# A layer of gated linear attention and SwiGLU: o of three heads in four turned through DRAM and by VectorE's 32 by 32 blocks instead of on TensorE

## The chip, the cores and the metric

One core of one Trainium2 chip. The metric is the device time of one execution in microseconds (us). Matrix products run on TensorE (PE in the profile), the rest on VectorE (DVE), ScalarE (ACT) and GpSimd (POOL); SyncE (SP) and ScalarE issue the DMA transfers.

## The reference

One layer on 2048 tokens of width 1024, in float32, cut to what the change touches:

```
hn = rmsnorm(h)
q, k, v, r, a_low = split(hn @ w_in)              # 4 heads, dk 128, dv 256
log_a = log_sigmoid(a_low @ w_a2 + b_a) / 16      # cumulated in chunks of 64 tokens
o = scores(q, k, decays) @ v + (q * decays) @ state      # by chunks, state carried on
o = rmsnorm(o of each head) * silu(r)
h = h + o.reshape(seq, 1024) @ w_out
h = h + (silu(g) * u) @ w_down      with g, u = split(rmsnorm(h) @ w_gu)
out = rmsnorm(h)
```

## The kernel before, in words

Numbers are kept as two float32r parts, hi and lo, and a product takes three matmuls (`three`, lines 735 to 737). The mixer goes over NB = 4 blocks of T = 512 tokens, each over H = 4 heads; then two stages of seven-product schemes make the feed-forward layer. The change lies in the mixer, which lasts until about 890 us, but for a few lines at the very end.

Weights of the mixer come through a ring: a block has 16 rounds of four units of 128x512. SP loads `raw` by pairs of units (`load_pair`, issue on line 405), each pair after GpSimd has split the same pair of the round before. GpSimd makes `ring_hi` and `ring_lo` of a unit (lines 660 and 663) after TensorE has used that unit of the round before. Head hd has rounds 3 hd (q and k columns), 3 hd + 1 and 3 hd + 2 (v and r, two halves); rounds 12 to 15 are w_out.

TensorE's order for heads 0 to 2: `make_scores` (k turned, past and future scores), the second half of v and r as four `vr_unit`s, the q columns of the next head, then, after the silu of r has read the banks (`r_silu`), `use_scores` with two units of the next head's v and r between, the k columns, `vr_unit` 2, `turn_o` (eight transposes of `og` into banks 6 and 7, line 878), `vr_unit` 3. Head 3 has no next head: `use_scores` follows on v and r, needing only the first `v_done`, and its `turn_o` lies inside the product with w_out.

VectorE's order for one head (`head`, from line 1685): k_lo, two predicated copies into `scores` (line 1698), scores_lo, the work of `under_vr`, state_in of the first tile (line 1708), two v_lo, the gate, the states, `under_o`, the root, four `og` tiles (line 1729); then `scale_qk` of the next head (lines 1611 to 1617) and `turned_o_lo`. ScalarE's order: k_hi, two copies into `scores`, scores_hi, `under_vr`, two v_hi, the silu of r (line 1210), the squares and the root, the decays, `turned_o_hi`. Under v and r of heads 1 and 2 lie, for blocks after the first, three operand splits of the block before: ScalarE issues two stores to xop (line 1161), splits three granules into three `x_stage` buffers, each after that buffer's last store has landed, and VectorE makes their low parts. Under v and r of head 3 lie, but for the last block, four squares of the next x on ScalarE, a root, and one scaled tile on VectorE. Between heads all orders are written out by hand; every engine goes strictly in its own.

SP also loads x of the next block in head 3 (line 461, blocks 1 and 2, after a wait for all xop stores) and the first feed-forward weights in heads 1 and 2 of block 3 (line 421).

```
def load_pair(i, p, parts):
    if i > 0:
        sp.wait_ge(unit_split[2 * p], i)
        sp.wait_ge(unit_split[2 * p + 1], i)
```

## Time and profile before

| what | value |
|---|---|
| median of 3 runs | 2199.96 us (2193.34 to 2200.28) |
| the profiled execution's own time | 2198.29 us |
| its span | 2196.6 us |
| granted TensorE clock, mean | 0.997 |
| TensorE busy | 2149.8 us |
| VectorE, ScalarE, GpSimd busy | 1384.1, 823.6, 1630.0 us |

The span goes from the first to the last instruction of the program. A row of a timeline has start, duration, engine and line, operation, what is written and read, and in brackets the idle time of its engine before it with what ended it. Merged rows have a count; their duration is that of the whole run of them.

### The profile page before, as it was taken

The page shows a single profiled execution, that of the slowest core. Times are in us where ns is not written, and L with a number is a line of the kernel's source. Part 1 is how long each engine was busy: PE and PEld are TensorE (multiplying, and loading weights), DVE is VectorE, ACT ScalarE, POOL GpSimd, SP SyncE. Part 2 cuts the span into 40 slices and gives each one's busy share as a digit, 9 for nine tenths or more (in the row PEclk, how much of TensorE's full clock was granted, in tenths as well). Part 3 has the DMA queues.
Part 4 walks back from the last instruction along what each step waited for, and adds up shares of the span by engine and source line. Part 5 has one row for each costly group of instructions (what it writes and reads, how often), then busy time and mean ns, then how long its engine had stood idle before and what let it go on. Part 6 is the DMA issues. An engine that isn't in the chain of part 4 may idle for free.

```text
span 2196.6 us, 27842 instructions
## 1 busy us (share of the span) xinstructions
PE 2149.8 (98%) x9922; PEld 1776.9 (81%) x9922; DVE 1384.1 (63%) x1800; ACT 823.6 (37%) x1461; POOL 1630.0 (74%) x1294
## 2 busy tenths in 40 slices
PE   8999999999999999999999998999999999999997
PEld 6888888778878888778888877888888878888885
DVE  6445644554455453378787855757667567978786
ACT  4333433343344333344444433443434422142223
POOL 7646675667566765788888878888888887878784
PEclk9999999999999999999999999999999999999999
DMA  6222354335433655745545458443434588759782
GB/s 187 77 67 87 121 186 121 119 114 189 123 131 110 200 162 201 259 158 201 182 175 192 161 206 344 151 166 135 171 132 174 206 308 311 282 214 359 262 320 105
DMA packets 225545, 404.75 MB, mean 184 GB/s; under 512 B 17184, under 2 KB 156448, under 8 KB 216448
## 3 DMA queue, kind: packets, MB, share of 16 engines
q1 hardware_dynamic: 190448, 360.44, 46.0%
q10 hardware_dynamic: 34960, 42.54, 5.8%
q8 instruction: 79, 1.29, 0.2%
q14 instruction: 58, 0.48, 0.1%
HBM read 273.94 MB, written 128.97 MB: 183 GB/s over the span
## 4 chain that ended last, share of the span: by engine, by line
PE 60%; DVE 3%; POOL 2%; issue 1%; DMA 1%; ACT 1%; SPq 0%; ACTq 0%; POOLq 0%; DVEq 0%
PE ps L735 20%; PE ps L737 20%; PE ps L736 20%; DVE acc L2012 1%; DMA x_op<-xop 1%; POOL ring_lo L663 1%; POOL ring_hi L660 0%; POOL w_op L672 0%; DMA raw<-in_gla_w_out 0%; DVE xs L1540 0%; PE ps L870 0%; DVE acc L1979 0%; SPq L473 0%; DMA raw<-in_gla_w_in 0%; DVE p_sum L2012 0%
## 5 line engine op out<-in xcount | busy, mean ns | idle before, releaser
L672 POOL TENSOR_TENSOR w_op<-w_raw,w_op 128x512 fp32r<-128x512 f32 x330 | 482.7, 1474 | 112.3 <-ACT w_op L1085 109.2
L735 PE MATMUL ps<-x_op,w_op 128*128 128x512 f32 x1232 | 480.9, 390 | 9.2 <-DMA x_op<-xop 3.3
L737 PE MATMUL ps<-x_op,w_op 128*128 128x512 f32 x1232 | 480.1, 390 | 0.0
L736 PE MATMUL ps<-x_op,w_op 128*128 128x512 f32 x1232 | 479.8, 389 | 0.0
L660 POOL TENSOR_SCALAR ring_hi<-raw 128x512 fp32r<-128x512 f32 x256 | 177.3, 693 | 293.8 <-issue 168.2
L663 POOL TENSOR_TENSOR ring_lo<-raw,ring_hi 128x512 fp32r<-128x512 f32 x256 | 351.7, 1374 | 21.3
L1085 ACT ACTIVATE w_op<-w_raw 128x512 fp32r<-128x512 f32 x330 | 202.6, 626 | 378.2 <-POOL w_raw L690 147.6
L735 PEld LDWEIGHTS ps<-x_op,w_op 128*128 128x128 f32 x1232 | 231.7, 188 | 59.5 <-issue 9.1
L737 PEld LDWEIGHTS ps<-x_op,w_op 128*128 128x128 f32 x1232 | 231.6, 188 | 48.4
L736 PEld LDWEIGHTS ps<-x_op,w_op 128*128 128x128 f32 x1232 | 231.8, 188 | 47.8
L735 PE MATMUL ps<-w_op,hid 128*128 128x512 f32 x616 | 240.8, 391 | 3.3 <-DVE acc L2012 0.9
L737 PE MATMUL ps<-w_op,hid 128*128 128x512 f32 x616 | 239.7, 389 | 0.0
L736 PE MATMUL ps<-w_op,hid 128*128 128x512 f32 x616 | 239.7, 389 | 0.0
L735 PE MATMUL ps<-ring_hi,xT_hi 128*128 128x512 f32 x512 | 203.5, 398 | 4.5 <-POOL ring_lo L663 4.5
L737 PE MATMUL ps<-ring_hi,xT_lo 128*128 128x512 f32 x512 | 200.3, 391 | 0.0
L736 PE MATMUL ps<-ring_lo,xT_hi 128*128 128x512 f32 x512 | 199.7, 390 | 0.0
L672 POOL TENSOR_TENSOR w_op<-w_t,w_op 128x512 fp32r<-128x512 f32 x112 | 169.1, 1509 | 29.3 <-ACT w_op L1085 29.3
L2012 DVE TENSOR_TENSOR acc<-acc,ps 128x512 f32<-128x512 f32 x224 | 145.8, 682 | 52.6 <-PE ps L737 51.2
L1085 ACT ACTIVATE w_op<-w_t 128x512 fp32r<-128x512 f32 x112 | 70.6, 630 | 209.4 <-POOL w_t L684 165.7
L735 PEld LDWEIGHTS ps<-w_op,hid 128*128 128x128 f32 x616 | 115.6, 188 | 31.8 <-issue 4.9
L737 PEld LDWEIGHTS ps<-w_op,hid 128*128 128x128 f32 x616 | 115.6, 188 | 24.1
L736 PEld LDWEIGHTS ps<-w_op,hid 128*128 128x128 f32 x616 | 115.6, 188 | 23.6
(206 smaller groups left out, 3992.3 us busy)
## 6 DMA issues: line engine op xcount, KB each, us to landing
hop<-stage SPq DMA_DIRECT2D x154, 512.0 KB, 2.9
hid<-hop SPq DMA_DIRECT2D x70, 1024.0 KB, 9.6
raw<-in_gla_w_in SPq DMA_DIRECT2D x192, 256.0 KB, 3.3
w_raw<-in_ffn_w_gu SPq DMA_DIRECT2D x176, 256.0 KB, 4.0
w_raw<-in_ffn_w_down SPq DMA_DIRECT2D x88, 256.0 KB, 4.5
xop<-x_stage ACTq DMA_DIRECT2D x42, 512.0 KB, 3.5
x_op<-xop SPq DMA_DIRECT2D x36, 512.0 KB, 8.6
raw<-in_gla_w_out SPq DMA_DIRECT2D x64, 256.0 KB, 3.1
```

The source lines that it names most:

```text
L660: pool.tensor_scalar(ring_hi[:, u, :], raw[:, p, u % 2, :], 1.0, 0.0, ALU.mult, ALU.add).then_inc(unit_hi, 1)
L663: pool.tensor_tensor(ring_lo[:, u, :], raw[:, p, u % 2, :], ring_hi[:, u, :].bitcast(F32), ALU.subtract).then_inc(unit_split[u], 1)
L672: pool.tensor_tensor(shaped(q, tile[:, 1, :]), source(q, i), shaped(q, tile[:, 0, :]).bitcast(F32), ALU.subtract).then_inc(op_ready[i], 1)
L735: pe.matmul(out, l_hi, r_hi, start=first, stop=False, skip_group_check=more)
L736: pe.matmul(out, l_hi, r_lo, start=False, stop=False, skip_group_check=more)
L737: return pe.matmul(out, l_lo, r_hi, start=False, stop=last, skip_group_check=more)
L1085: return act.activation(dst, src, ACT.Copy)
L2012: ins = dve.tensor_tensor(dst, dst, bank, ALU.add)
```

## The change

`turn_o` is kept for head 3 alone. For heads 0, 1 and 2, SP stores the four og tiles (512 KB) to `og_kept` in DRAM and loads them back as `og_by_32`: partition 32 i + s holds, for each of 16 groups of 32 tokens, 64 numbers of token s, in pieces of 256 bytes, with one DMA for each i. VectorE then turns 32 by 32 blocks, two instructions of 128x512, into `oT` (in SBUF, the place of `oT_lo`), and sets `oT_blocks`. The split into hi and lo comes one head later, 1024 columns in one instruction, behind the copies into scores on ScalarE and behind scores_lo on VectorE. Columns of o are taken by twos (2 p + j), and the rows of w_out likewise. The store of head hd is issued before the first column pair of head hd + 2, the load behind that pair; for head 2 both stand before the pairs of w_out. `make_scores` waits for og in place of oT_lo. Besides, the first pair of a round goes before x of the next block, and at the end of the kernel some variances, roots and scaled tiles come later in VectorE's and ScalarE's order (on VectorE the variance, root and scaled tile of the third tile each one gather later; the scaled one behind the last gather).

```diff
-    o_w = w_out[0].rearrange("(k p) n -> p k n", p=P)
+    o_w = w_out[0].rearrange("(h p j) n -> h j p n", p=P, j=2)
...
+        oT = sb("oT", OT, [P, KV, T])
...
+        og_by_32 = sb("og_by_32", OG, [P, T // 32, DV // 4])
...
+        og_kept = nc.dram_tensor("og_kept", [T, DV], F32)
...
-            def load_vr(i, hd, n):
+            def load_vr(i, hd, n, next_x=None):
                 for p in range(2):
...
+                    if p == 0 and next_x is not None:
+                        wait_operands(next_x - 1)
+                        load_x(next_x)
 
             def load_out(i, n):
-                half, k2 = divmod(n, KV // 2)
-                rows(i, n % 2, o_w, 2 * k2, half * HALF)
+                half, hd = divmod(n, H)
+                load_pair(i, n % 2, [(raw[:, n % 2, j, :], o_w[hd, j, :, half * HALF:half * HALF + UNIT])
+                                     for j in range(2)])
+
+            def store_og(b, hd):
+                sp.wait_ge(og_done, NT * (b * H + hd + 1))
+                sp.dma_start(og_kept[:, :].rearrange("(t p) c -> p t c", p=P), og[:, :, :]).then_inc(og_stored, 16)
+
+            def load_og(b, hd):
+                sp.wait_ge(og_stored, 16 * (b * (H - 1) + hd + 1))
+                by_32 = og_kept[:, :].rearrange("(m s) (i c) -> i s m c", s=32, i=4)
+                for i in range(4):
+                    sp.dma_start(og_by_32[32 * i:32 * i + 32, :, :], by_32[i]).then_inc(og_loaded, 16)
 
             for b in range(NB):
                 for hd in range(H):
                     i = b * ROUNDS + 3 * hd
+                    if hd >= 2:
+                        store_og(b, hd - 2)
                     columns(i, 0, q_w, hd * DK)
+                    if hd >= 2:
+                        load_og(b, hd - 2)
                     columns(i, 1, k_w, hd * DK)
                     load_vr(i + 1, hd, 0)
...
-                    if hd == H - 1 and 0 < b < NB - 1:
-                        wait_operands(b)
-                        load_x(b + 1)
-                    load_vr(i + 2, hd, 1)
+                    load_vr(i + 2, hd, 1, b + 1 if hd == H - 1 and 0 < b < NB - 1 else None)
...
+                store_og(b, H - 2)
+                load_og(b, H - 2)
                 i = b * ROUNDS + ROUND_OUT
...
-                    pool.wait_ge(oT_done, 2 * NB * H)
+                    pool.wait_ge(oT_done, 2 * NB)
...
-                if n > 0:
-                    pe.wait_ge(oT_lo_done, 2 * n)
-                if n > 0 and n % H == 0:
+                if n % H > 0:
+                    pe.wait_ge(og_done, NT * n)
+                elif n > 0:
+                    pe.wait_ge(oT_lo_done, (H + 1) * (n // H))
                     pe.wait_ge(xf_done, 2 * NT * (n // H) - 1)
...
-                        ins = pe.transpose(ps[:, 6 + j, t * P:(t + 1) * P], og[:, t, j * P:(j + 1) * P], ident[:, :])
+                        ins = pe.transpose(ps[:, 6 + j, t * P:(t + 1) * P], og[:, t, j::2], ident[:, :])
...
                     vr_unit(i + 4, 0, 2)
-                    turn_o(n)
                     vr_unit(i + 4, 0, 3)
...
+                if hd > 0:
+                    turned_o_hi(b, hd - 1)
                 act.wait_ge(scores_ready, 2 * (n + 1))
...
             def turned_o_hi(b, hd):
-                n = b * H + hd
+                act.wait_ge(oT_blocks, (H - 1) * b + hd + 1)
+                parts = slice(2 * hd, 2 * hd + 2)
+                split_hi(oT_hi[:, parts, :], oT[:, parts, :]).then_inc(oT_hi_done, 1)
...
-            for j in range(4):
+            for j in range(3):
...
+            square_of(1, 3, 0)
+            square_of(1, 3, 1)
+            root_of(1, 2)
+            square_of(1, 3, 2)
+            square_of(1, 3, 3)
             root_of(1, 3)
+            last_scaled(2)
             last_scaled(3)
...
                 split_lo(scores_lo[:, :, :], scores[:, :, :], scores_hi[:, :, :]).then_inc(scores_split, 1)
+                if hd > 0:
+                    turned_o_lo(b, hd - 1)
                 under_vr()
...
+            def turn_o_blocks(b, hd):
+
+                dve.wait_ge(og_loaded, 16 * 4 * ((H - 1) * b + hd + 1))
+                for j in range(2):
+                    ins = dve.transpose(oT[:, 2 * hd + j, :].rearrange("p (m s) -> p m s", s=32),
+                                        og_by_32[:, :, j::2])
+                ins.then_inc(oT_blocks, 1)
+
             def turned_o_lo(b, hd):
...
+                dve.wait_ge(oT_hi_done, (H + 1) * b + hd + 1)
+                parts = slice(2 * hd, 2 * hd + 2)
+                split_lo(oT_lo[:, parts, :], oT[:, parts, :], oT_hi[:, parts, :]).then_inc(oT_lo_done, 1)
...
                     head(b, hd, operands_under_vr(hd), operands_under_o(hd))
                     scale_qk(b * H + hd + 1)
-                    turned_o_lo(b, hd)
+                    turn_o_blocks(b, hd)
...
-                            if (l, i) in ((2, 1), (2, 6), (3, 3)):
+                            if (l, i) in ((2, 1), (2, 6), (3, 4)):
```

## Rows read from the trace of the kernel before

**Rows 1.** Page, busy time and share of each engine, instructions

```profile
PE 2149.8 (98%) x9922; PEld 1776.9 (81%) x9922; DVE 1384.1 (63%) x1800; ACT 823.6 (37%) x1461; POOL 1630.0 (74%) x1294
```

**Rows 2.** Waits of TensorE, 60 to 880 us: total, times, longest

```profile
PE ps L735 <- POOL ring_lo L663: 6.1, 11, 2.2
```

**Rows 3.** Timeline of TensorE at a turn_o: start, length, line, idle before

```profile
303.52 0.39 PE L736 MATMUL ps<-ring_lo,xT_hi 128*128 128x512 f32 x1
303.75 0.40 PE L737 MATMUL ps<-ring_hi,xT_lo 128*128 128x512 f32 x1
...
305.10 0.39 PE L736 MATMUL ps<-ring_lo,xT_hi 128*128 128x512 f32 x1
```

**Rows 4.** All instructions of tile og on TensorE: min/median/max ns

```profile
L878 PE MATMUL ps<-ident,og x128: 270/272/275, 84.0 to 867.3; 128*128 128x128 f32 x128
```

**Rows 5.** Timeline of VectorE, block 1, end of head 0 and head 1

```profile
299.72 1.66 DVE L1729 SCALAR_TENSOR_TENSOR og<-ps,rstd,r_gate 128x256 f32<-128x256 f32 x4
...
303.08 0.68 DVE L1617 TENSOR_TENSOR qk_scaled<-ps,ef 128x512 f32<-128x512 f32 x1
...
310.21 0.93 DVE L1698 COPY_PREDICATED scores<-future,ps 64x256 f32<-64x256 int32 x2 [0.59 <-ACT scores L1198]
...
318.30 1.37 DVE L1708 TENSOR_SCALAR state_in<-state,e_odd,e_even 128x256 f32<-128x256 f32 x1
...
321.58 0.69 DVE L1516 TENSOR_TENSOR v_lo<-ps,v_hi 128x512 fp32r<-128x512 f32 x1 [0.67 <-ACT v_hi L1085]
```

**Rows 6.** Timeline of SP's queue in six stretches: first issue, issue time, count

```profile
164.68 0.88 SPq L405 DMA_DIRECT2D raw<-in_gla_w_in  x2
...
303.66 0.88 SPq L405 DMA_DIRECT2D raw<-in_gla_w_in  x2
...
308.82 2.25 SPq L405 DMA_DIRECT2D raw<-in_gla_w_in  x2
...
345.46 4.84 SPq L405 DMA_DIRECT2D raw<-in_gla_w_in  x4
...
383.78 3.14 SPq L405 DMA_DIRECT2D raw<-in_gla_w_in  x4
...
752.25 2.00 SPq L421 DMA_DIRECT2D w_raw<-in_ffn_w_gu  x4
```

**Rows 7.** Landings of the xop stores of ScalarE's queue, 260 to 460 us

```profile
DMA to landing us min/median/max: 2.9/3.7/5.4
```

**Rows 8.** Landings of SP's raw loads, 260 to 440 us

```profile
DMA to landing us min/median/max: 2.7/3.3/8.1
```

**Rows 9.** Timeline of ScalarE, block 1, heads 1 and 3

```profile
311.17 0.63 ACT L1085 ACTIVATE scores_hi<-scores 128x512 fp32r<-128x512 f32 x1 [1.05 <-DVE scores L1698]
...
323.64 1.03 ACT L1210 ACTIVATE r_gate<-ps 128x1024 f32<-128x1024 f32 x1
...
393.55 0.63 ACT L1085 ACTIVATE scores_hi<-scores 128x512 fp32r<-128x512 f32 x1 [1.04 <-DVE scores L1698]
```

**Rows 10.** Timeline of TensorE, first product of use_scores, block 1, heads 1 and 3

```profile
326.19 0.28 PE L735 MATMUL ps<-v_hi,k_hi 128*128 128x256 f32 x1
...
405.78 0.28 PE L735 MATMUL ps<-v_hi,k_hi 128*128 128x256 f32 x1
```

**Rows 11.** Timelines of ScalarE and TensorE, block 0, head 3

```profile
172.19 0.63 ACT L1085 ACTIVATE scores_hi<-scores 128x512 fp32r<-128x512 f32 x1 [1.05 <-DVE scores L1698]
...
182.16 0.39 PE L735 MATMUL ps<-v_hi,k_hi 128*128 128x256 f32 x1 [0.24 <-DVE v_lo L1516]
```

**Rows 12.** Timeline of GpSimd, block 1, head 3

```profile
392.53 0.62 POOL L660 TENSOR_SCALAR ring_hi<-raw 128x512 fp32r<-128x512 f32 x1 [6.58 <-DMA raw<-in_gla_w_in]
```

**Rows 13.** Timeline of ScalarE, last scaled tile

```profile
2190.94 1.15 ACT L1476 ACTIVATE acc<-acc,rstd 128x1024 f32<-128x1024 f32 x1 [0.82 <-DVE rstd L1535]
```

**Rows 14.** Busy us (x) by stretch: PE, PEld, DVE, ACT, POOL, PEclk, DMA share, GB/s

```profile
1345.00:1349.80 4.80, 1.54 (x8) 0.97 (x7) 1.88 (x4) 1.67 (x3) 4.72 (x4) 1.00 1.03 419
1349.80:1353.20 3.40, 3.40 (x10) 2.63 (x9) 3.15 (x3) 2.68 (x5) 3.40 (x3) 0.50 1.03 418
```

More of the change, by code:

```diff
@@ L195, in gla_layer @@
                              "oT_lo_done"))
+        og_stored, og_loaded, oT_blocks = sem("og_stored"), sem("og_loaded"), sem("oT_blocks")
         wo_done, wo_added = sem("wo_done"), sem("wo_added")
@@ L410, in columns @@
                                   w[:, 4 * u:4 * u + 4, start:start + P]) for u in range(2)])
-            def rows(i, p, w, k, start):
-                load_pair(i, p, [(raw[:, p, u, :], w[:, k + u, start:start + UNIT]) for u in range(2)])
             def load_quad(q):
@@ L952, in _ @@
                 pe.wait_ge(r_silu, n + 1)
-                pe.wait_ge(oT_lo_done, 2 * n)
+                pe.wait_ge(oT_lo_done, (H + 1) * b + H - 1)
                 more = b < NB - 1
@@ L959, in _ @@
                     if m == 6:
-                        pe.wait_ge(oT_lo_done, 2 * n + 2)
+                        pe.wait_ge(oT_lo_done, (H + 1) * (b + 1))
                     if m == KV and more:
@@ L1226, in turned_o_hi, with turned_last_hi @@
             def turned_o_hi(b, hd):
-                n = b * H + hd
+                act.wait_ge(oT_blocks, (H - 1) * b + hd + 1)
+                parts = slice(2 * hd, 2 * hd + 2)
+                split_hi(oT_hi[:, parts, :], oT[:, parts, :]).then_inc(oT_hi_done, 1)
+            def turned_last_hi(b):
                 for j in range(2):
-                    act.wait_ge(oT_done, 2 * n + j + 1)
+                    act.wait_ge(oT_done, 2 * b + j + 1)
                     act.nop(nofuse=True)
-                    split_hi(oT_hi[:, 2 * hd + j, :], ps[:, 6 + j, :]).then_inc(oT_hi_done, 1)
+                    split_hi(oT_hi[:, KV - 2 + j, :], ps[:, 6 + j, :]).then_inc(oT_hi_done, 1)
             def square_next(b):
@@ L1296, in _ @@
                     head(b, hd, operands_under_vr(hd), operands_under_o(hd))
-                    turned_o_hi(b, hd)
                 if b < NB - 1:
@@ L1301, in _ @@
                     turned_hi(b + 1, 1, 4)
-                    turned_o_hi(b, H - 1)
+                    turned_last_hi(b)
                     turned_hi(b + 1, 2, 4)
@@ L1314, in _ @@
                     head(b, H - 1, lambda: None, load_turned_operands)
-                    turned_o_hi(b, H - 1)
+                    turned_last_hi(b)
                     load_op(0, 2)
@@ L1850, in _ @@
                     turned_lo(b + 1, 1, 4)
-                turned_o_lo(b, H - 1)
+                turned_last_lo(b)
                 if more:
@@ L2059, in _ @@
                         if B == 1:
-                            if (l, i) in ((2, 1), (2, 6), (3, 3)):
-                                variance_fin(1, ((2, 1), (2, 6), (3, 3)).index((l, i)))
-                            elif (l, i) in ((2, 2), (3, 1), (3, 4)):
-                                root_fin(1, ((2, 2), (3, 1), (3, 4)).index((l, i)))
-                            elif (l, i) in ((2, 3), (3, 2), (3, 5)):
-                                scale_fin(1, 0, ((2, 3), (3, 2), (3, 5)).index((l, i)))
+                            if (l, i) in ((2, 1), (2, 6), (3, 4)):
+                                variance_fin(1, ((2, 1), (2, 6), (3, 4)).index((l, i)))
+                            elif (l, i) in ((2, 2), (3, 1), (3, 5)):
+                                root_fin(1, ((2, 2), (3, 1), (3, 5)).index((l, i)))
+                            elif (l, i) in ((2, 3), (3, 2), (3, 6)):
+                                scale_fin(1, 0, ((2, 3), (3, 2), (3, 6)).index((l, i)))
                         elif (l, i) == (2, 1):
```

6 lines of the change are left out of this document (3 added, 3 removed).

## The prediction

> **What bounds the kernel now.** I read the share of each engine first: TensorE is busy in 2149.8 of 2196.6 us [rows 1], so time comes off only where TensorE has less to do, and is lost wherever it is made to wait. Then its waits in the mixer stage (60 to 880 us), where the whole change lies: the longest total is 6.1 us, for GpSimd's split of weights [rows 2]. Every other engine is early. The question is therefore twofold: how much TensorE work goes, and whether something that was early becomes late.
>
> **What is removed.** turn_o goes in heads 0, 1 and 2 of four blocks, 12 times eight transposes. In block 1, head 0, the product before it starts at 303.75 and the second one behind it at 305.10 [rows 3]. Products of 512 columns stand 0.23 us apart (303.52 to 303.75), so 0.45 of these 1.35 us would be there anyway: 0.90 us a turn, and all 16 turns look alike (270 to 275 ns a transpose) [rows 4]. 12 x 0.90 = 10.8 us, the whole possible gain of this part.
>
> **What is put in its place, step by step, in block 1 between heads 0 and 1.**
> - The last og tile ends at 301.38 [rows 5]. SP comes to the store only behind the pair of raw loads that it issues at 303.66 for 0.88 us [rows 6], so the store leaves at 304.5. 512 KB from SBUF to DRAM land in 2.9 to 5.4 us, 3.7 in the middle [rows 7]: about 308.2. No loss yet.
> - The load back stands behind the column pair of head 2, and that pair waits for GpSimd's split: 308.82 [rows 6]. With 0.9 us for the pair the four loads leave from 309.7, one each 0.43 us, the last about 311.0. A 256 KB load lands 2.7 to 8.1 us after its issue, 3.3 in the middle [rows 8]. The new ones have 128 KB each in pieces of 256 bytes, which no row shows; by their bytes they would be quicker, by the number of pieces (512 each, as many as the column loads have) not. I take 3.2: landed at 314.2. Low 2.2, high 4.5.
> - VectorE has stood in turn_o_blocks since scale_qk ended at 303.76 [rows 5], 10 us. The two turns of 128x512 have no row. Below it cannot be under VectorE's pace of about 0.6 us for 512 columns (the one at 303.08 takes 0.68 and ends 0.1 into the next) [rows 5]; above I put 1.4, what 256 columns took at worst while GpSimd was at work (state_in, 1.37) [rows 5]. I take 0.65, nearest to the operations of the same shape: done at 315.5.
> - Behind it in VectorE's order stand k_lo (0.6) and two predicated copies (0.93, at 310.21 before) [rows 5]. ScalarE's scores_hi, at 311.17 before [rows 9], comes at 317.1, 5.9 us late. ScalarE is blocked as well, in turned_o_hi, and so are the two xop stores that it issues beside scores_hi.
> - From scores_hi to state_in VectorE took 7.13 us (311.17 to 318.30) [rows 5, 9]. That stretch is not work but round trips: the next x_stage splits wait for exactly those two stores to land. So it does not shrink: state_in at 324.2 and, with 0.7 to 1.37 for it and 1.3 for the two v_lo, v_done at about 326.4. Here the new 1024 wide splits of o (1.1 us on ScalarE, 1.3 on VectorE) are free; they lie in the waits.
> - The silu of r_gate ended 2.4 us behind the second v_lo (322.27 to 324.67) [rows 5, 9]: now 328.8 to 329.3. TensorE must have it before use_scores, which began at 326.19 without any wait [rows 10] and could begin at 325.3 now. Before, the silu had 1.5 us to spare; now it is 3.7 us late. TensorE starts 2.8 us later than before, in spite of the 0.9 us saved.
>
> **The other eleven places.** Blocks 1 to 3 have the operand splits under heads 1 and 2. In head 2 the column pair leaves 3.9 us behind the pair before it and not 5.2 (two pairs from 345.46 to 350.30, the last 0.92 long) [rows 6]: the turn ends 1.2 earlier there and 1.6 are lost. Blocks 1 and 2: 2 x (2.8 + 1.6) = 8.8. In block 3 four w_raw loads, 2.0 us of issue and 1 MB, stand before the store [rows 6]; the store then lands after the column pair has left, I take 1.5 us more for each: 7.4. Heads 1 and 2 of block 0 have no operand splits: there the two turns end about 13 us behind the first product of vr_unit 2, and with 1.6 to scores_hi and 3.4 for scores_lo, the split of o and state_in VectorE reaches v_lo at about 18, when vr is done: no loss, 2 x 0.9 gained. Head 3 of block 3 has no work under vr either: 0.9 gained.
>
> Head 3 of blocks 0 to 2 has the four squares, the root and a scaled xs between scores_hi and v_lo, a chain without slack: in block 0 TensorE already waits for v_lo, at 182.16 [rows 11]. There SP issues its raw pair at 164.68 [rows 6], the store follows at 165.6, lands at 169.3, the loads leave until 170.6 and land at 173.8, turns 175.1, scores_hi 176.7 in place of 172.19 [rows 11]: **4.5 us lost**. In blocks 1 and 2 the store also stands behind 2 MB of xs. Before, a raw pair issued at 383.78 landed at 392.5 [rows 6, 12]. The store, issued at about 386.9, then lands near 394.5, the loads at 398.7, the turns end at 400.0 and scores_hi starts at 401.6 instead of 393.55 [rows 9]; 8.0 late less 0.4 that were to spare before use_scores at 405.78 [rows 10]: **7.6 lost**, twice. Were the store not held up, it would be 3.5.
>
> **Small parts.** load_vr lets the first pair of round 11 pass the wait for xop: this takes away a wait of 2.2 us [rows 2] that lies inside the 7.6 already. As TensorE is late, some other waits for GpSimd vanish: -1.5. At the end, VectorE's scaled tile stood before the last gather, and ScalarE's last_scaled(2), 1.15 us like the one shown [rows 13], before the last three squares; without them the last scaled tile, at 2190.94 before, waits for the previous one on ScalarE: -1.2 (0 to -2). The new row order of w_out, the PSUM bank and GpSimd's wait cost nothing: same bytes, same counts.
>
> **The clock.** In the stage behind, TensorE worked at half clock for 3.4 us [rows 14] right after a stretch in which it was busy 1.5 of 4.8 us; that costs 1.7 us. The waits in head 3 of blocks 0 to 2 become 6 to 11 us long, so I count 3 x 1.7 = 5.1, with up to 15 more if the shorter ones count too. The Trainium skill, "TensorE: Matmul & The Clock Gate", Part 1, agrees in kind: an array that has idled is gated to half rate.
>
> **Sum.** -2.7 + 4.5 + 15.2 + 8.8 + 7.4 - 1.5 - 1.2 + 5.1 = +35.6 us on the profiled 2198.29, or 2233.9; the median of the three runs is 1.7 above that run, so 2234 or 2235.
>
> The Trainium skill, "VectorE: DVE Perf Modes", "The three transpose paths", has 311 ns for 128x128 in two-byte numbers on VectorE; four of those would be 1.24 us a turn in place of 0.65, and the sum about 11 us higher. No row here shows the operation.
>
> **The rivals.**
> - *The round trip is hidden* (faster). All engines but TensorE have idle time, and VectorE waited 2.3 us before k_lo anyway. Then 10.8 + 1.2 us come off: 2188. In heads 1 and 2 it decides at the end of the second turn: it must come before about 312 (325.3 less 2.4, 1.3, 0.7, 7.1 and 1.6). But the first of the four loads can't leave before 309.7 and the last before 311.0, so the landing and both turns would have 1 us. I give 0.11, for a misreading of the order of the queues.
> - *Half hidden*: every unknown at its low end (loads land in 2.2, turns 0.6, the store past xs unhindered, no clock loss). Heads 1 and 2 lose 0 to 1.5 each, head 3 2.3, 4 and 4: +8, 2207. With a bit less it is no change: 0.05 for within 0.3%.
> - *The clock falls at every longer wait and small pieces are slow*: loads in 4.5, turns 1.4: some 2.8 us more in nine places and 15 for the clock: 2275. 0.15.
> - *GpSimd becomes the bound*, because the raw loads share their queue with 12 MB more: its unit takes 2.0 us against TensorE's 2.7, and TensorE is held up elsewhere, so this adds little beside the rest.
>
> **The numbers.** Forecast 2234, chance 0.69 with its own range 2212 to 2258. The rival above adds 0.15 to slower, giving 0.84; same 0.05; faster 0.11 (0.3%, 6.6 us, is about what can be told from no change). The range leaves out the faster case and the far end: 2204 to 2265.
>
> **What would show it.** Right: no L878 in heads 0 to 2; VectorE idle some 10 us before each turn, ended by the og load; ScalarE idle for the turn; TensorE waiting 3 to 4 us before use_scores for r_gate, 6 to 11 us in head 3 for v_lo. Wrong: the og load leaving before the column pair's turn, or TensorE without new waits.

## The result and the profile after

| | before | after |
|---|---|---|
| median of 4 runs | 2198.41 us (2193.34 to 2200.28) | 2256.49 us (2255.58 to 2257.14) |
| span of the profiled execution | 2196.6 us | 2254.7 us |
| mean granted TensorE clock | 0.997 | 0.981 |

The ratio is 1.0271, 95% interval 1.0258 to 1.0284: 58 us slower. The forecast of 2234 us was right in direction and 22 us short; the time lies inside its range of 2204 to 2265.

The page, busy time of each engine, after. It answers to [rows 1]:

```profile
PE 2158.1 (96%) x9826; PEld 1784.0 (79%) x9826; DVE 1399.3 (62%) x1812; ACT 821.8 (36%) x1449; POOL 1634.9 (73%) x1294
```

TensorE has 96 matmuls fewer, the 12 turns of eight, and yet its busy time rose by 8.3 us: some of its work ran at half clock. VectorE has 15 us more to do, which says nothing about the 58 us.

The waits of TensorE, 60 to 1000 us, kernel after (total, times, longest). They answer to [rows 2], where 6.1 us for GpSimd was the longest total (7.8 by this longer window):

```profile
PE ps L756 <- ACT r_gate L1233: 33.3, 6, 7.5
PE ps L756 <- DVE v_lo L1549: 27.7, 4, 9.9
PE ps L756 <- POOL ring_lo L684: 2.2, 7, 0.7
```

Six waits of 4.5 to 7.5 us for the silu of r (heads 1 and 2 of blocks 1 to 3), three of 7.0 to 9.9 for v_lo (head 3 of blocks 0 to 2) and one of 1.2 (head 3 of block 3) make up 61 us, where there was next to nothing. The wait for GpSimd, in turn, has shrunk.

All instructions on tile oT, kernel after (min/median/max ns), then what they waited for and who waited:

```profile
L1772 DVE STREAM_TRANSPOSE oT<-og_by x24: 669/693/712, 95.5 to 906.0; 128x512 f32<-128x512 f32 x24
L1549 DVE TENSOR_TENSOR oT_lo<-oT,oT_hi x12: 1212/1630/2312, 99.7 to 909.8; 128x1024 fp32r<-128x1024 f32 x12
...
  DMA og_by<-og_kept: 138.3, 12
...
  ACT oT_hi L1106: 88.8, 12
```

The turn itself is quick. What is slow is what it waits for: VectorE stands 138.3 us in all for the load of og, 11.5 us each time, and ScalarE stands behind it.

Block 1, head 1, kernel after, followed from the last og tile to TensorE. First VectorE's timeline (start, length; in brackets the idle time and what ended it), then SP's queue, ScalarE and TensorE. They answer to [rows 3], [rows 5], [rows 6], [rows 9] and [rows 10]:

```profile
306.80 1.66 DVE L1764 SCALAR_TENSOR_TENSOR og<-ps,rstd,r_gate 128x256 f32<-128x256 f32 x4
...
322.42 1.30 DVE L1772 STREAM_TRANSPOSE oT<-og_by 128x512 f32<-128x512 f32 x2 [11.57 <-DMA og_by<-og_kept]
...
326.89 2.31 DVE L1549 TENSOR_TENSOR oT_lo<-oT,oT_hi 128x1024 fp32r<-128x1024 f32 x1
...
333.53 0.70 DVE L1743 TENSOR_SCALAR state_in<-state,e_odd,e_even 128x256 f32<-128x256 f32 x1
```

```profile
311.66 0.47 SPq L510 DMA_DIRECT2D og_kept<-og  x1
315.89 0.92 SPq L413 DMA_DIRECT2D raw<-in_gla_w_in  x2
316.86 2.10 SPq L516 DMA_DIRECT2D og_by<-og_kept  x4
```

```profile
323.76 1.06 ACT L1106 ACTIVATE oT_hi<-oT 128x1024 fp32r<-128x1024 f32 x1 [7.45 <-DVE oT L1772]
325.17 0.63 ACT L1106 ACTIVATE scores_hi<-scores 128x512 fp32r<-128x512 f32 x1 [0.35 <-DVE scores L1731]
...
329.56 0.63 ACT L1106 ACTIVATE x_stage<-xf 128x512 fp32r<-128x512 f32 x1 [2.73 <-DMA xop<-x_stage]
...
331.61 0.63 ACT L1106 ACTIVATE x_stage<-x_sum 128x512 fp32r<-128x512 f32 x1 [1.41 <-DMA xop<-x_stage]
...
336.92 1.02 ACT L1233 ACTIVATE r_gate<-ps 128x1024 f32<-128x1024 f32 x1
```

```profile
313.78 0.60 PE L854 MATMUL ps<-ident,qk_scaled 128*128 128x128 f32 x4
...
338.00 0.58 PE L756 MATMUL ps<-v_hi,k_hi 128*128 128x256 f32 x1 [5.48 <-ACT r_gate L1233]
```

Read it as one chain: four loads issued between 316.86 and 318.96, landed at 322.4, two turns, k_lo and the scores, scores_hi, two xop buffers whose stores have to land first (2.73 and 1.41 of waiting), state_in, v_lo, silu, TensorE. No engine on it is busy for long; it is made of waits for transfers and of orders written out.

The clock of TensorE around that wait and around the one in head 3 (stretch, length, busy us (count) of PE, PEld, DVE, ACT, POOL, PEclk, DMA share, GB/s), kernel after:

```profile
332.00:334.50 2.50, 0.52 (x3) 0.10 (x1) 2.20 (x3) 1.32 (x3) 2.42 (x3) 1.00 0.86 211
334.50:341.30 6.80, 3.30 (x13) 3.12 (x14) 4.18 (x7) 3.34 (x4) 4.01 (x4) 0.50 0.80 267
...
423.20:436.80 13.60, 6.01 (x24) 5.65 (x25) 6.52 (x14) 7.70 (x14) 4.99 (x5) 0.50 0.27 77
```

After TensorE had been busy 0.52 of 2.5 us it was granted 0.50 of its speed (the lower of its two levels, 1.2 GHz) for 6.8 us, and of those it worked 3.3; around the wait in head 3 it was 13.6 us. Each of the nine long waits has such a stretch, 3.4 to 13.7 us long, 71.7 us together. Up to its last 15 us the kernel before had only one, of 3.4 us, in the stage behind [rows 14].

### The profile page after: what moved, and what is told of

It is laid out like the page before. It is cut to its first block, busy times and chain, and to the rows that moved or that the text cites. A ratio compares the mean times of both kernels' runs of the same rounds, so it can differ in the third digit from the quotient of the medians.

```text
span 2254.7 us, 27685 instructions
## 1 busy us (share of the span) xinstructions
PE 2158.1 (96%) x9826; PEld 1784.0 (79%) x9826; DVE 1399.3 (62%) x1812; ACT 821.8 (36%) x1449; POOL 1634.9 (73%) x1294
## 4 chain that ended last, share of the span: by engine, by line
PE 57%; DVE 4%; DMA 2%; issue 1%; POOL 1%; SPq 1%; ACT 1%; ACTq 0%; DVEq 0%; POOLq 0%
PE ps L756 19%; PE ps L757 19%; PE ps L758 19%; DVE acc L2059 1%; DMA og_kept<-og 1%; DMA x_op<-xop 1%; DMA og_by<-og_kept 0%; SPq L425 0%; POOL ring_lo L684 0%; PE ps L892 0%; POOL w_op L693 0%; DVE xs L1573 0%; DVE acc L2026 0%; DMA raw<-in_gla_w_out 0%; DVE p_sum L2059 0%
## 5 line engine op out<-in xcount | busy, mean ns | idle before, releaser
L684 POOL TENSOR_TENSOR ring_lo<-raw,ring_hi 128x512 fp32r<-128x512 f32 x256 | 356.5, 1392 | 21.4
```

Of the source, the lines that this page charges most:

```text
L684: pool.tensor_tensor(ring_lo[:, u, :], raw[:, p, u % 2, :], ring_hi[:, u, :].bitcast(F32), ALU.subtract).then_inc(unit_split[u], 1)
```

## The experiments

Each ratio is against the kernel before as it ran on the same chip in the same series. Kernels that ran in different series are compared by these ratios.

**1. The turn moved off the path.** VectorE turns o behind v_lo instead of ahead of k_lo (in head 3 behind the states), and the splits follow behind the silu and the states.

```diff
@@ VectorE, head
-                if hd > 0:
-                    turned_o_lo(b, hd - 1)
                 under_vr()
...
+                        if 0 < hd < H - 1:
+                            turn_o_blocks(b, hd - 1)
                         if hd < H - 1:
                             gate_r(n)
...
+                elif hd > 0:
+                    turned_o_lo(b, hd - 1)
                 under_o()
@@ VectorE, loop over heads
                     scale_qk(b * H + hd + 1)
-                    turn_o_blocks(b, hd)
```

> All of the change, but the 32 by 32 turns and the split of o stand where their engines have time: in heads 1 and 2 VectorE turns behind the second v_lo, ScalarE splits behind the silu, VectorE's low part comes behind the states; in head 3 all three come behind the states and the root, and the product with w_out waits for this head's part only before its fifth unit. The kernel before took 2198.4 us, the changed one 2256.5. Theory A, the loss is VectorE and ScalarE standing still in their own order for the og load: the load lands 7.5 to 12 us behind the start of make_scores, v_lo ends 14.7 behind it, so no wait is left; 12 turns of TensorE at 0.9 us and the tail come off: 2187 us (2184 to 2191). Theory B, what costs is the new work and traffic itself (1 MB of DMA a head, turns and 1024 wide splits beside GpSimd): 2200 us or more, with TensorE waiting for GpSimd's units or for r_gate.

Measured: 2201.88 us against 2197.42, ratio 1.0023 (1.0014 to 1.0032). The time lies in B's range, and B's sign is there too: TensorE waits 11.4 us for GpSimd's units, 6.1 before. But the waits for r_gate are gone, and with them 54 of the 58 us. The same transfers, turns and splits are still there, so what cost the time was where the rest of the chain stood behind the load. TensorE's waits now, 60 to 880 us:

```profile
PE ps L756 <- POOL ring_lo L684: 11.4, 10, 4.4
PE ps L756 <- DVE v_lo L1552: 4.6, 3, 2.1
PE ps L786 <- DVE xT_lo L1552: 3.8, 3, 1.3
```

The longest, 4.4 us for GpSimd, is in block 3, and SP's queue tells why:

```profile
753.15 2.00 SPq L425 DMA_DIRECT2D w_raw<-in_ffn_w_gu  x4
755.20 0.47 SPq L510 DMA_DIRECT2D og_kept<-og  x1
757.38 1.21 SPq L413 DMA_DIRECT2D raw<-in_gla_w_in  x2
761.46 2.74 SPq L516 DMA_DIRECT2D og_by<-og_kept  x4
```

The store waits behind four weight transfers, SP then stands for its landing with a raw pair behind it, and GpSimd splits late.

**2. The trip left out.** VectorE turns blocks of og itself; nothing is stored or loaded, so that o is turned only within blocks and the output is not the layer's.

```diff
             def store_og(b, hd):
-                sp.wait_ge(og_done, NT * (b * H + hd + 1))
-                sp.dma_start(og_kept...).then_inc(og_stored, 16)
+                pass
@@ VectorE, turn_o_blocks
-                                        og_by_32[:, :, j::2])
+                                        og[:, :, :].rearrange("p t (q c) -> p (t q) c", c=64)[:, :, j::2])
```

> The changed kernel without the way through DRAM: no store, no load; VectorE turns the blocks of og itself, at the same place in its order. (Left out: o of heads 0 to 2 is turned only within 32 by 32 blocks, not across them.) Theory A, the wait for the trip is the whole loss: VectorE starts the turn right behind scale_qk, some 2 us before k_lo can start, so TensorE waits nowhere new: 2187 us (2184 to 2191), TensorE's waits for r_gate and v_lo near 0. Theory B, part of the loss is the turns and wide splits on VectorE's and ScalarE's path: 1.3 us of turns and 1.6 of the low part in front of v_lo in head 3, where the chain has no slack, would show as 1 to 2 us in three places or more: 2190 to 2200.

Measured: 2184.43 us against 2197.42, ratio 0.9940 (0.9927 to 0.9954), at the low end of theory A. With the turn where the change has it but without the trip, the loss becomes a gain. This run takes away the transfers together with the wait for them; experiment 1 keeps the transfers and loses 54 of the 58 us all the same. The two together show that the loss is the wait for the round trip.

The gain of 13.0 us is 6.6 short of the 10.8 of the turns and the 8.8 of the rest of the change (experiment 4). TensorE's waits, 60 to 880 us, have nearly all of it:

```profile
PE ps L752 <- POOL ring_lo L680: 6.8, 9, 1.7
PE ps L752 <- DVE v_lo L1545: 3.1, 3, 1.6
```

In experiment 4 they are 2.7 and 0.7 us, 6.5 less. So these two waits come without any transfer of og.

**3. The xop stores ahead of the wait.** ScalarE issues its two stores before it waits for the turn.

```diff
+                if b > 0 and 0 < hd < H - 1:
+                    result_store(b - 1, 5 * hd - 2)
+                    result_store(b - 1, 5 * hd - 1)
                 if hd > 0:
                     turned_o_hi(b, hd - 1)
```

> The changed kernel, but in heads 1 and 2 of blocks 1 to 3 ScalarE issues the two xop stores before it waits for the turn, instead of behind scores_hi. Theory A (prediction): the 8.4 us from scores_hi to state_in are round trips of these two stores; with the stores landed early, only VectorE's own work is left in it, 1.6 for the low part of o and some 3 for three splits, so each of six places gains 2 to 3 us and its share of the clock loss: 2238 us (2232 to 2244). Rival: that stretch is VectorE's work, and the stores would have landed anyway: 2252 to 2257.

Measured: 2267.83 us, ratio 1.0324 (1.0309 to 1.0340): slower than the change itself, and outside both expectations. The stretch from scores_hi to state_in did shrink, in block 1, head 1, from 8.36 to 6.80 us and in the six places together from 47.2 to 41.8, but the og load was hit. SP, then VectorE, block 1, head 1:

```profile
318.01 3.80 SPq L516 DMA_DIRECT2D og_by<-og_kept  x4
```

```profile
327.17 1.31 DVE L1772 STREAM_TRANSPOSE oT<-og_by 128x512 f32<-128x512 f32 x2 [15.86 <-DMA og_by<-og_kept]
...
335.72 1.08 DVE L1549 TENSOR_TENSOR x_stage<-x_sum,x_stage 128x512 fp32r<-128x512 f32 x1 [0.59 <-ACT x_stage L1106]
336.73 0.70 DVE L1743 TENSOR_SCALAR state_in<-state,e_odd,e_even 128x256 f32<-128x256 f32 x1
```

Four issues took 3.80 us in place of 2.10, and the turn began 5.4 us after their end in place of 3.5. ScalarE had issued its two stores at 315.78, 2.2 us before. All six places with such stores have their turns later than in the change, by 2.2 to 4.3 us counted from the k transposes; the six without have them where they were, within 0.5. So 5.4 us are gained in the six stretches and 17.0 lost ahead of them. The stores are the only thing that was moved; that they and the loads slow each other where they meet is the reading of it, and how is not shown.

**4. and 7. What else the change holds.** First the kernel before with the change's order of loads (a raw pair goes ahead of x of the next block) and its tail, all turns on TensorE; then with the tail alone.

```diff
             def load_vr(i, hd, n, next_x=None):
                 for p in range(2):
                     ...
+                    if p == 0 and next_x is not None:
+                        wait_operands(next_x - 1)
+                        load_x(next_x)
```

> The kernel before with the two small parts of the change alone: the first pair of round 11 is loaded before x of the next block, and the last variances, roots and scaled tiles come later. Theory A: TensorE's 2.2 us wait for GpSimd at 394 us and 0.7 at 617 go, and the tail gains 1.2: 2194.5 us (2193 to 2197). Rival: VectorE's chain in head 3 (the four squares, the scaled xs, v_lo) then ends last and takes back what GpSimd's wait gave: 2197.

> This is the kernel before with one part of the change alone: the order of the last squares, roots and scaled tiles on ScalarE and VectorE at the end of the program. The run with this part and the earlier load of x together (turns still on TensorE) gained 8.8 us. Theory A: the tail gives the 1.2 us that the prediction put on it, 2196.2 (2195 to 2197), and the load order the other 7.6, through the heads 1 of blocks 2 and 3. Rival B: the tail gives half or more of the gain, 2193 or below.

Measured: 2188.65 us against 2197.42, ratio 0.9958 (0.9945 to 0.9970), for both; 2195.48 against 2196.60, ratio 0.9992 (0.9983 to 1.0000), for the tail. Both together gained more than either theory had. The tail gives 1.1 us (0 to 3.7 by its interval), which fits the 1.2 of the forecast, and the order of loads about 7.6 (6.8 when both were run again, experiment 11). TensorE's waits for GpSimd, 60 to 880 us, of both together and, second, with the tail alone:

```profile
PE ps L735 <- POOL ring_lo L663: 2.7, 9, 0.4
```

```profile
PE ps L735 <- POOL ring_lo L663: 5.3, 11, 1.9
```

Less than half of the 7.6 us shows as such waits. From head 3 of blocks 1 and 2 to the next block, counted between the k transposes, it takes 98.6 and 97.9 us in place of 101.5 and 100.5. In block 1 the whole of this is waits that go, 2.2 us for ring_lo and 0.7 for state_in; in block 2 such waits, with those for v_lo, are 1.8 of the 2.6 us. The rest wasn't followed further.

**5. TensorE kept running.** Matmuls without use fill the waits, so that only the clock changes.

```diff
                     column_units(i + 3, 0, ps[:, 0, :])
+                    if b > 0 and hd > 0:
+                        run_on(18, 0)
                     pe.wait_ge(r_silu, n + 1)
...
                 vr_last_units(first + ROUND_OUT - 1)
+                if b < NB - 1:
+                    run_on(24, 0)
                 use_scores(n, None)
```

> This is the changed kernel with matmuls added whose results go unused, placed where TensorE otherwise stands: 18 of 512 columns into bank 1 ahead of the wait for the silu in heads 1 and 2 of blocks 1 to 3, and 24 ahead of the use of the scores in head 3 of blocks 0 to 2 (at 0.2265 us each 4.1 and 5.4 us). Nothing else moves. Theory A: of the 58 us that the change costs, 48 are waits for the late chain (load, turns, k_lo, scores_hi, state_in) and 10 are TensorE at half clock after each wait. Then the waits stay, the half-clock stretches in the first 880 us mostly go, and the time is 2244 to 2250. Rival B: the half clock falls inside the waits, where it costs nothing, and all 58 us are chain: 2255 to 2260, at the time of the changed kernel. Rival C: VectorE and ScalarE are themselves later because TensorE's products at half clock come later to them, so that the chain shortens too: below 2240.

Measured: 2249.48 us against 2196.60, ratio 1.0238 (1.0220 to 1.0256), with a mean clock of 0.993 in place of 0.981. The kernel is 52.9 us above the one before by the medians and 52.3 by the ratio, the change 58.1 and 59.6. So keeping TensorE running gives back 5 to 7 us (2 to 12 by the intervals of the two ratios), and the rest of the loss is still there as time without useful products. The time lies in A's range, but A had 10 us for the clock. The traces tell why it is less. Outside the stretches from the k transposes to use_scores the change is 10.3 us longer than the kernel before and this one 0.4 us shorter: there the clock costs some 10 us. The stretches themselves are 3.2 us longer together than in the change; why is open. The clock still fell in four places, for 17.1 us in place of 71.7.

**6. The loads ahead of the column pair.**

```diff
-                    columns(i, 0, q_w, hd * DK)
                     if hd >= 2:
                         load_og(b, hd - 2)
+                    columns(i, 0, q_w, hd * DK)
                     columns(i, 1, k_w, hd * DK)
```

> This is the changed kernel with the four loads of og issued ahead of the first column pair of head 2 and 3 (in place of between the two pairs). Theory A: the loads wait only for the store to land, which it does some 3 us after its issue 2.1 us before the k transposes begin, so that they are issued about 2 us earlier, and each of the nine places with a late turn gives about 2 us back: 2238 to 2243. Rival B: SyncE now stands for the store with the column pair behind it, the raw halves and GpSimd come later by up to 3 us in heads 2 and 3, and this takes back what was gained: 2252 to 2260, with waits of TensorE for GpSimd's ring_lo above the 2.2 us of the changed kernel. (Heads 1 of a block take their turn of the head before at head 2's place in the queue either way.)

Measured: 2252.37 us, ratio 1.0245 (1.0228 to 1.0261): 2 us gained by the medians and 6 by the ratios, hardly clear of the intervals, and in B's range. Block 1, head 1, still goes as A says: the loads leave 1.3 us earlier counted from the k transposes, its turns begin 2.4 us earlier, and TensorE 3.1. But in block 3 the raw pair behind them is late, as B says. TensorE's wait for GpSimd, 60 to 1000 us, is 7.3 us in place of 2.2:

```profile
PE ps L756 <- POOL ring_lo L684: 7.3, 12, 2.3
```

**8. The late turn, mended twice.** The weight transfers of block 3 go one head later, and o of head 2 is split behind the first turned tile of the next x.

```diff
@@ SP
-                    if hd in (1, 2) and b == NB - 1:
-                        sp.wait_ge(lc_ready, NB + 1)
-                        load_quad(hd - 1)
...
                     load_vr(i + 1, hd, 0)
+                    if hd >= 2 and b == NB - 1:
+                        sp.wait_ge(lc_ready, NB + 1)
+                        load_quad(hd - 2)
```

> This is the run with the turn moved behind v_lo, with two repairs. In block 3 the two transfers of the next stage's weights are issued one head later, so that the store and loads of og don't queue behind them; and at the end of a block the low half of head 2's o comes behind the first turned tile of the next x on VectorE. Theory A: the waits named in that run go: 4.7 + 3.1 us for GpSimd in block 3 with about 3 us of half clock after them, and three of 1.7 us for the turned tiles; 2201.9 - 7.8 - 3 - 5 = 2186 (2184 to 2190), level with the 2188.7 of the kernel with the turns on TensorE. Rival B: the GpSimd waits come from the four small loads on the queue whatever stands beside them: 2194 to 2198.

Measured: 2189.92 us against 2196.60, ratio 0.9969 (0.9957 to 0.9981): level with all turns on TensorE (below, 0.9967), as A has it. Twelve of the sixteen `turn_o` have left TensorE, and nothing is gained by it: within a block most heads come 0.9 us sooner, and from head 3 to the next block it takes 101.1 to 101.2 us in place of 97.9 to 98.6.

**9. The wide split alone moved** from behind scores_lo to behind the states.

```diff
-                if hd > 0:
-                    turned_o_lo(b, hd - 1)
                 under_vr()
...
+                if hd > 0:
+                    turned_o_lo(b, hd - 1)
                 under_o()
```

> This is the changed kernel with one instruction per head moved: the low half of the turned o on VectorE (128x1024, 1.63 us in the median, of two inputs in SBUF) goes from behind scores_lo to behind the state's steps. The turn, the loads and ScalarE stay. It tests the term that was mis-sized: from the start of scores_hi to state_in block 1 head 1 took 8.36 us in the changed kernel where the prediction kept the 7.13 of before. Theory A: this split is the difference, so that state_in comes 1.2 to 1.6 us earlier in the nine places that wait; with the half clock behind shorter waits the time falls by 11 to 16 us, to 2241 to 2246. Rival B: state_in waits in those heads for the three x operands' own chain (ScalarE, VectorE, stores), in which the split has room: 2254 to 2257.

Measured: 2264.89 us, ratio 1.0306 (1.0293 to 1.0320), slower than either expects. TensorE's waits, then VectorE in block 1, head 1:

```profile
PE ps L756 <- ACT r_gate L1233: 33.4, 6, 6.8
...
PE ps L756 <- DVE oT_lo L1549: 8.9, 4, 2.3
```

```profile
331.09 1.01 DVE L1549 TENSOR_TENSOR x_stage<-xf,x_stage 128x512 fp32r<-128x512 f32 x1 [2.64 <-ACT x_stage L1106]
333.19 0.69 DVE L1549 TENSOR_TENSOR x_stage<-x_sum,x_stage 128x512 fp32r<-128x512 f32 x1 [1.09 <-ACT x_stage L1106]
333.80 0.71 DVE L1741 TENSOR_SCALAR state_in<-state,e_odd,e_even 128x256 f32<-128x256 f32 x1
```

The waits for r_gate are what they were: B is right about the mechanism. Where the split was, VectorE now idles 2.64 us for the store, and from scores_hi to state_in it is 7.75 us instead of 8.36. That gain is this place's alone: over the six such places the stretch comes to 47.3 us, 47.2 in the change. The 8.9 us more are the split's new place, where the product with w_out in head 3 waits for it: my edit added a wait that neither theory had counted.

**10. and 11. The late turn once more, and all turns on TensorE again beside it.** To experiment 8 two orders are added. The og loads come behind the second column pair, and the first scaled tile of the next x behind v_lo.

```diff
                     columns(i, 0, q_w, hd * DK)
-                    if hd >= 2:
-                        load_og(b, hd - 2)
                     columns(i, 1, k_w, hd * DK)
+                    if hd >= 2:
+                        load_og(b, hd - 2)
@@ VectorE
                 def next_under_vr():
                     norm_next(b)
-                    scale_next(b, 0)
                 def next_under_o():
+                    scale_next(b, 0)
```

> This is the second run with the late turn, with two more orders changed. The four loads of og come behind the second column pair of the head in place of between the two (the late turn leaves them the time), so that the raw halves reach GpSimd earlier; and the first scaled tile of the next x on VectorE comes behind v_lo in head 3 (it took 2.21 us in block 0 beside GpSimd in place of 1.28, and TensorE stood 2.4 us for the v_lo behind it). Theory A: GpSimd is then no later than with the turns on TensorE, the three waits of 1.7, 2.0 and 1.5 us in heads 1 and the one of 2.4 go, and removing 24 of 32 turns shows as the 0.9 us a place that TensorE saves (12 places, less 2 for what VectorE adds): 2180 to 2184, below the kernel with the turns on TensorE. Rival B: the waits in heads 1 come from VectorE's wide instructions of two SBUF inputs, beside which one of GpSimd takes 1.0 us longer (2.28 in place of 1.30), and not from the loads; then only the 2.4 goes and the time stays at 2187 to 2189, level with it.

> This is the kernel with all turns on TensorE and only the change's load order and tail, run again beside the late turns on the same chip: 2187 to 2190, ratio 0.9945 to 0.9970. If the late turn gains anything of its own, it stands below this by more than 2 us; if the turns are worth nothing off TensorE, within 1.

Measured: 2199.85 us against 2197.24, ratio 1.0009 (1.0001 to 1.0018), and 2189.35 us, ratio 0.9967 (0.9955 to 0.9980). The second is where it was expected, the first is 10 us above both theories: both edits failed. SP and TensorE's waits, 60 to 880 us, of the late turn:

```profile
317.91 3.65 SPq L516 DMA_DIRECT2D og_by<-og_kept  x4
321.65 6.39 SPq L413 DMA_DIRECT2D raw<-in_gla_w_in  x4
```

```profile
PE ps L756 <- POOL ring_lo L684: 9.7, 10, 2.6
PE ps L786 <- DVE xT_lo L1552: 5.6, 3, 1.9
...
PE ps L756 <- DVE v_lo L1552: 0.7, 1, 0.7
```

The wait for v_lo went (3.1 to 0.7 us), but VectorE then came late with the turned tiles (5.6 us); and at their new place the four loads hold SP for 3.65 us just where the next raw pair is due.

**12. Two heads in four.** As 8, but heads 2 and 3 are turned by TensorE.

```diff
                     vr_unit(i + 4, 0, 2)
+                    if hd == H - 2:
+                        turn_o(n)
                     vr_unit(i + 4, 0, 3)
@@ SP
-                store_og(b, H - 2)
-                load_og(b, H - 2)
```

> This is the second run with the late turn, but only o of heads 0 and 1 goes through DRAM; heads 2 and 3 are turned by TensorE as before. So head 3 of a block holds none of the added work of VectorE. Measured against the kernel with all turns on TensorE (2187.4 us of span), the late turn of three heads gave 0.92 us for each step from one head to the next of the same block where nothing else bounds it, nothing in the step from head 1 to 2 of blocks 1 to 3 (41.3 us against 41.2: GpSimd's work), and lost 3.3 us at the end of each of blocks 0 to 2, where VectorE's turns, its wide split and steps of 1.0 to 1.5 us in place of 0.4 beside GpSimd hold up TensorE. Theory A: those 3.3 us go with head 2's turn, the gains of 5 steps stay (heads 0 and 1 of block 0, head 0 of blocks 1 to 3): 2189.0 - 5 x 0.9 = 2184.5 (2183 to 2187). Rival B: the shift of GpSimd against VectorE by itself costs the 3.3 us at the block's end, whoever turns head 2: 2193 to 2196.

Measured: 2186.20 us against 2197.45, ratio 0.9948 (0.9935 to 0.9960), the shortest of all that compute the layer. From head 3's k transposes to the next block's it takes 98.0 us in place of 101.2: A is right that the loss sat in head 3. Its interval overlaps with that of all turns on TensorE (0.9945 to 0.9970 and 0.9955 to 0.9980), so a gain from the turns themselves (2.5 to 3.4 us by the medians) is not shown. It also has the weight transfers of block 3 one head later, which the kernel with all turns on TensorE has not; what that is worth alone wasn't measured.

## Why the prediction was right, and where it was short

The mechanism was the one that happened: the turn waits for the round trip, k_lo, the scores and scores_hi wait for the turn, and TensorE waits for r_gate or v_lo. The waits for r_gate were forecast at 3 to 4 us and are 4.5 to 7.5; those for v_lo, forecast at 6 to 11, are 7.0 to 9.9. Counted from the end of the last og tile in block 1, head 1 (301.38 before, 308.46 after), in us:

| step | forecast | measured |
|---|---|---|
| the store leaves | 3.1 | 3.2 |
| four loads issued | 8.3 to 10.0 | 8.4 to 10.5 |
| the turns begin | 12.8 | 14.0 |
| the turns have ended | 14.1 | 15.3 |
| scores_hi begins | 15.7 | 16.7 |
| state_in begins | 22.8 | 25.1 |
| TensorE begins use_scores (24.8 before) | 27.6 | 29.5 |

Both turns took 1.30 us, exactly the 2 x 0.65 taken from neighbouring rows. The Trainium skill, "VectorE: DVE Perf Modes", "The three transpose paths", would have made it 2.5 by my estimate (eight times its 311 ns for 128x128 in bf16); here the trace has 0.69 for one turn of 128x512 in float32, and the measurement decides.

**Term one that was mis-sized: the landing.** I took 3.2 us from the last issue; it was 4.0 here (start of the last issue, 318.4, to 322.42), and the issues themselves took 2.10 in place of 1.72. Between the two bounds I gave, 2.2 and 4.5. With the queue in front of the store it is the larger part of the error. Counted from the k transposes, the forecast has the turns at 7.5 us in head 1 and 6.3 in head 2, and 1.5 more in block 3; in the six places they come 11.1 us later than that together. 4.2 of it is block 3, head 2, where the store left 3.6 us later than in the blocks before, against the 1.5 of the forecast.

**Term two: "it does not shrink".** It grew: 8.36 us in place of 7.13 in block 1, head 1, and 47.2 in place of 41.5 over the six places. "Not work but round trips" was half right. With the wide split of o moved away (experiment 9) VectorE stands for the stores instead, and the six stretches stay at 47.3; so the split had room there, but for 0.6 us in block 1, head 1, where it took 2.31 us beside GpSimd. With the stores landed early (experiment 3) the stretch is still 6.80 us, and between scores_lo and state_in VectorE then idles for 0.59 of it: that is VectorE's own work. The two chains are nearly equally long, and taking away one leaves the other. What made both longer than before was not separated.

By place, loss of TensorE from its k transposes to use_scores, less the 0.90 us a turn saved (in block 1, head 1, 338.00 - 313.78 - 18.59 - 0.90 = 4.7, with 18.59 from the same two instructions of the kernel before):

| place | forecast | measured |
|---|---|---|
| block 0, heads 1 and 2 | -1.8 | -1.6 |
| block 0, head 3 | 4.5 | 5.9 |
| blocks 1 and 2, heads 1 and 2 | 8.8 | 16.8 |
| blocks 1 and 2, head 3 | 15.2 | 13.4 |
| block 3, heads 1 and 2 | 7.4 | 12.9 |
| block 3, head 3 | -0.9 | 0.4 |
| clock, waits gone, tail | 2.4 | 10.3 |
| sum | 35.6 | 58.1 |

The places with operand splits carry the error, 13.5 us in six places: the two terms above, 1.9 us together in block 1, head 1, and in block 3 the queue in front of the store. Head 3 of blocks 0 to 2, where no xop store is in the chain, came out at 19.3 us where 19.7 were forecast, and this is partly luck: block 0 lost 1.4 us more and the other two 1.8 less. In block 1 SP stood 6.1 us behind the store's issue and not 7.6, but the four issues then took 3.04 us and not 1.72. (By its own terms the forecast should have had the loads there landed at 399.0, not 398.7.)

**Term three: the clock.** I counted it in three places, as 5.1 us. It fell in nine, in the shorter waits too. The line with the clock, the waits gone and the tail was forecast at 2.4 us and came to 10.3; where TensorE was kept running (experiment 5) it came to -0.4. So by these two traces the clock is about 10 us of it, and of these 5 to 7 came back in the whole time.

**The side that I passed over.** I gave GpSimd's waits 1.5 us and took the order of loads for part of head 3. Alone it is worth about 7 us (experiments 4, 7 and 11). The change hides it, since TensorE waits longer there for something else.

**The rivals.** "The round trip is hidden" was rejected because the loads could not leave in time; experiment 1 shows that it can be hidden, by an order in which nothing waits for it. "GpSimd becomes the bound" looked small, and is one of two things that take the gain back once the waits are gone. With the late turn of experiment 8, heads of the same block follow each other after 39.64 us and not 40.56, but from head 1 to head 2 of blocks 1 to 3, where GpSimd also has the sums, it is 41.3, 41.6 and 41.1 us against 41.0, 40.7 and 41.4: TensorE's saved 0.9 turns into waits of 1.2 to 1.7 us for ring_lo. The transfers are not what makes them: without the trip (experiment 2) the same steps take 41.6 us, with waits of 1.7. These three steps give back 3.6 of the 10.8 us. The three from head 3 to the next block give back 9.0, with TensorE waiting for VectorE's state_in, v_lo and oT_lo (3.9, 3.1 and 1.7 us in the mixer, 0.4, 0.7 and none with all turns on TensorE).

## What to carry to other kernels

Work taken off the busiest engine is worth its time only if what takes its place has no consumer in the written order before its transfer has landed: put the wait behind everything that doesn't need it, and look at which engines stand in turn behind that wait. Where a stretch holds both round trips and an engine's work, price both chains, for the longer one counts, and add the clock for every wait, not only for the long ones. And once the wait is hidden, ask what the engine just relieved waits for next; here VectorE at the end of each block took back 9.0 of the 10.8 us, and GpSimd most of the rest.

## What the runs showed that I had not expected

**VectorE and GpSimd stop each other.** Head 3 of block 1, first the late turn of experiment 8, VectorE and GpSimd, then VectorE and GpSimd with all turns on TensorE:

```profile
404.80 0.98 DVE L1744 TENSOR_SCALAR state_in<-state,e_odd,e_even 128x256 f32<-128x256 f32 x1
...
406.27 1.52 DVE L1744 TENSOR_SCALAR state_in<-state,e_odd,e_even 128x256 f32<-128x256 f32 x1
```

```profile
404.35 1.28 POOL L684 TENSOR_TENSOR ring_lo<-raw,ring_hi 128x512 fp32r<-128x512 f32 x1
...
406.34 1.30 POOL L684 TENSOR_TENSOR ring_lo<-raw,ring_hi 128x512 fp32r<-128x512 f32 x1
```

```profile
405.27 0.44 DVE L1714 TENSOR_SCALAR state_in<-state,e_odd,e_even 128x256 f32<-128x256 f32 x1
...
406.20 0.87 DVE L1714 TENSOR_SCALAR state_in<-state,e_odd,e_even 128x256 f32<-128x256 f32 x1
```

```profile
405.64 1.27 POOL L663 TENSOR_TENSOR ring_lo<-raw,ring_hi 128x512 fp32r<-128x512 f32 x1
```

A state_in of 0.4 us that begins within a ring_lo, or less than 0.1 us ahead of one, ends 0.15 us after it: at 405.78 after 405.63, at 407.79 after 407.64, at 407.07 after 406.91, and so in all 22 such cases of the first trace and all 19 of the second. The one at 405.27 began 0.37 us ahead of its ring_lo and took 0.44. So the same instruction takes 0.44 or 1.52 us by how the two engines stand to each other, and moving the turns shifts that. The other way round, the wide split of o (two inputs in SBUF) had a ring_hi beside it in the kernel after that took 1.59 us and not 0.62:

```profile
328.09 1.59 POOL L681 TENSOR_SCALAR ring_hi<-raw 128x512 fp32r<-128x512 f32 x1
```

The Trainium skill, "SBUF — State Buffer", "Who interferes with whom", says that the two engines share a pair of SBUF ports that one instruction holds to its end, and that a VectorE instruction with two inputs in SBUF contends with one of GpSimd that reads SBUF. It also names tensor_scalar, which state_in is, among the kinds that can take the shared pair. The trace agrees with both: 0.15 us from the end of the one to the end of the other. The split before the change had one input in PSUM, and took 0.68 to 0.69 us for 512 columns all 32 times; the wide one takes 1.2 us for 1024 at its shortest and 2.3 at its longest.

**Small loads suffer from a neighbour.** The four loads of og in pieces of 256 bytes took 2.10 us to issue and landed 3.5 us after the last one's end; with two stores just ahead of them on another queue 3.80 and 5.4 (experiment 3). In the six places with such stores the issues took 2.7 to 3.8 us, and 1.9 to 2.1 in the change.

**The clock falls after short waits too, but not after each.** With the tail alone (experiment 7) it went to 0.50 for 3.4 us after a wait of 1.9 us, at 392.6; in experiment 10 a wait of 2.6 us, at 328.8, had no such stretch behind it.
